# Memory key and value projections between the steps of the cross-attention, two probability buffers

## What is computed

```python
mk_p = jnp.einsum('bmd,ldk->lbmk', mem_prompt, w_mk)   # memory keys of the prompt, an output too
mv_p = jnp.einsum('bmd,ldk->lbmk', mem_prompt, w_mv)   # memory values of the prompt, an output too
...
def memory_attention(x, mem_k, mem_v, w_mq, w_mo):
    q = (x @ w_mq).reshape(bsz, T, MEM_HEADS, MEM_HD)            # 4 heads of 256
    s = jnp.einsum('bthd,bmhd->bhtm', q, mem_k) * (MEM_HD ** -0.5)
    p = jax.nn.softmax(s, axis=-1)
    o = jnp.einsum('bhtm,bmhd->bthd', p, mem_v)
    return o @ w_mo
...
x = layer_norm(DN_ALPHA * x + mix, ln_g[l, 0], ln_b[l, 0])
x = layer_norm(DN_ALPHA * x + memory_attention(x, mem_k[l], mem_v[l], w_mq[l], w_mo[l]), ln_g[l, 1], ln_b[l, 1])
x = layer_norm(DN_ALPHA * x + hier_moe(x, ...), ln_g[l, 2], ln_b[l, 2])
```

## Time and profile before

| | us |
|---|---|
| median of 3 runs | 1953.09 |
| lowest, highest | 1949.16, 1953.87 |
| profiled execution | 1948.43 |
| its span, first to last instruction | 1946.7 |
| PE, DVE, ACT busy in the span | 1541.0, 455.4, 297.1 |
| layer 0, end of the mixer's output projection to start of the attention's | 169.6 |
| layer 1, the same | 170.6 |

### The profile page before, as it was taken

One profiled execution on the slowest core, in us unless ns is written; L12 is line 12 of the kernel. 1 busy time (PEld: TensorE's weight loads), 2 busy tenths in 40 slices (PEclk: granted clock), 3 DMA queues, 4 the chain that ended last, 5 costly groups with the idle time before them and its releaser, 6 DMA issues.

```text
span 1946.7 us, 32778 instructions
## 1 busy us (share of the span) xinstructions
PE 1541.0 (79%) x14532; PEld 1001.6 (51%) x14532; DVE 455.4 (23%) x969; ACT 297.1 (15%) x530; POOL 107.1 (6%) x232
## 2 busy tenths in 40 slices
PE   8997899787967766777599878998779677567773
PEld 6766447545644534455275664466456355344550
DVE  0338400414111110111310664104141110101103
ACT  1233102302000000000122321113020000000001
POOL 3123100000000000000000321000000000000000
PEclk9987899886999889888699768998879988898886
DMA  9431333582999999999923323425828999999993
GB/s 343 146 130 52 113 140 110 207 364 76 384 418 417 421 422 420 418 417 420 351 87 130 101 82 114 151 108 187 362 99 357 418 416 423 422 419 419 417 421 120
DMA packets 118175, 536.42 MB, mean 276 GB/s; under 512 B 5614, under 2 KB 23054, under 8 KB 101648
## 3 DMA queue, kind: packets, MB, share of 16 engines
q1 hardware_dynamic: 113600, 519.98, 67.1%
q0 software_dynamic: 2704, 7.95, 1.3%
q10 hardware_dynamic: 1728, 6.29, 0.9%
HBM read 521.71 MB, written 12.49 MB: 274 GB/s over the span
## 4 chain that ended last, share of the span: by engine, by line
PE 48%; DMA 31%; DVE 8%; SPq 7%; ACT 3%; issue 2%; ACTq 0%; DVEq 0%; POOL 0%
PE ps L587 11%; DMA W<-in_w_gate 9%; DMA scr<-in_w_up 7%; SPq L393 7%; PE ps L633 6%; DMA W<-in_w_down 6%; PE ps L622 6%; PE ps L875 5%; DMA W<-in_w_up 4%; DMA scr<-in_w_down 4%; PE ps L859 3%; PE ps L602 2%; PE ps L715 2%; DVE scr L1274 2%; PE ps L884 2%
## 5 line engine op out<-in xcount | busy, mean ns | idle before, releaser
L875 PE MATMUL ps<-W,scr 128*32 128x128 f32 x6144 | 216.9, 303 | 76.0 <-issue 49.4
L875 PEld LDWEIGHTS ps<-W,scr 128*32 128x32 f32 x6144 | 192.0, 123 | 109.7 <-issue 69.1
L587 PE MATMUL ps<-XT,W 128*128 128x288 f32 x896 | 223.1, 412 | 3.3 <-ACT XT L995 2.8
L587 PEld LDWEIGHTS ps<-XT,W 128*128 128x128 f32 x896 | 172.0, 193 | 53.0 <-ACT XT L995 4.1
L884 PE MATMUL ps<-W,scr 128*32 128x512 f32 x768 | 118.0, 749 | 91.4 <-DMA W<-in_w_down 85.3
L859 PE MATMUL ps<-scr 128*128 128x128 f32 (+1 forms) x864 | 166.2, 326 | 0.9 <-DVE scr L1436 0.9
L1447 DVE TENSOR_TENSOR X<-X,ps 32x256 f32<-32x256 f32 x72 | 29.8, 414 | 526.9 <-PE ps L847 526.1
L859 PEld LDWEIGHTS ps<-scr 128*128 128x128 f32 (+1 forms) x864 | 126.9, 202 | 40.0 <-issue 11.0
L884 PEld LDWEIGHTS ps<-W,scr 128*32 128x32 f32 x768 | 23.7, 124 | 174.8 <-DMA W<-in_w_down 124.5
L622 PE MATMUL ps<-W,scr 128*128 128x512 f32 x256 | 110.3, 593 | 1.6 <-ACT scr L1023 1.6
L1157 ACT ACT_TABLE_LOAD x16 | 20.5, 1283 | 593.7 <-PE ps L875 593.7
(11 more groups left out here) (294 smaller groups left out, 1563.0 us busy)
## 6 DMA issues: line engine op xcount, KB each, us to landing
W<-in_w_gate SPq DMA_DIRECT2D x48, 2048.0 KB, 27.7
W<-in_w_up SPq DMA_DIRECT2D x48, 2048.0 KB, 31.0
W<-in_w_down SPq DMA_DIRECT2D x48, 2048.0 KB, 30.7
scr<-in_w_gate SPq DMA_DIRECT2D x16, 2048.0 KB, 24.0
scr<-in_w_up SPq DMA_DIRECT2D x16, 2048.0 KB, 29.1
scr<-in_w_down SPq DMA_DIRECT2D x16, 2048.0 KB, 37.1
scr<-in_cache_mem_k SPq DMA_DIRECT2D x16, 1024.0 KB, 6.9
scr<-in_cache_mem_v SPq DMA_DIRECT2D x16, 1024.0 KB, 5.9
```

What stands on the lines that cost most here:

```text
L587: last = mm(bank[:, 0:NT], w[:, k, c * P:(c + 1) * P], XT[:, k, :], start=(k == 0), stop=(k == KC - 1))
L875: last = mm(ps[j * CAP:(j + 1) * CAP, bank, e * P:(e + 1) * P], XG[:, k, e * CAP:(e + 1) * CAP], w[:, k, j * P:(j + 1) * P], start=(k == 0 ...
```

## The change

The order of the units becomes mq, mk, mv, mo, and the memory stage is planned after the queries. PE no longer runs the memory part as a whole: the four transposing jobs come after the queries, one key job after every second cached key, the prompt's keys are turned last, one value job follows the prompt scores, and three more lie between the first values. The transposed memory tokens go to `XT` (free once the queries are made), the new keys to `GB` (free once the norm is done), so the norm's next parameters are loaded later. The first three cache loads are issued at the end of the mixer, for which the mixer's output `o` moves out of their way. Each prompt tile has its probabilities in its own buffer, with its own small columns; ACT makes both tiles' exponentials before it copies anything of them out, and DVE does both maxima before the scalings.

```diff
-            for name in ("mk", "mv", "mq", "mo"):
+            for name in ("mq", "mk", "mv", "mo"):
...
+        PR = [KT0.rearrange("p k m -> p (k m)")[:, 0:MH * MEM].rearrange("p (h m) -> p h m", h=MH), PR1]
+        MEMT = XT[:, :, 0:MEM]
+        MK = GB
...
+            plan_xt(1 + 3 * l)
+            plan(("mq", l), *[("feat", f"mq{j}", c) for j in range(2) for c in range(4)])
             plan(("mem", l), *[("mt", i, h) for i in range(MT_) for h in range(2)])
             plan(("mem", l), *[("memtok", f"{w}{j}", i) for w in ("mk", "mv") for j in range(2) for i in range(MT_)])
-            plan_xt(1 + 3 * l)
-            plan(("mq", l), *[("feat", f"mq{j}", c) for j in range(2) for c in range(4)])
...
+                        sp.wait_ge(S("state_out"), count_at("state_out", l, 32 * HEADS))
+                        sp.wait_ge(S("rms"), count_at("rms", l, HEADS))
+                        for i in range(3):
+                            sp.dma_start(KV[i], caches[i]).then_inc(S(f"kv_in{i}"), 16)
...
+                for i in range(3, 2 * DB):
+                    if i < DB + 3:
+                        sp.wait_ge(S("kt_full"), count_at("kt_full", l, 4 * (i - 2)))
                     else:
-                        sp.wait_ge(S("pv_done"), count_at("pv_done", l, i - 3 - DB + 1))
+                        sp.wait_ge(S("pv_done"), count_at("pv_done", l, i - 2 - DB))
...
-                pool.wait_ge(S("pipe_free"), number(("mem", l)))
-                pool.dma_start(O["mem_k"][l, 0].rearrange("(i p) h d -> p i (h d)", p=P), KV[2]).then_inc(S("memk_out"), 16)
+                pool.wait_ge(S("pipe_free"), mem_done(l, MEM_JOBS // 2 - 1))
+                pool.dma_start(O["mem_k"][l, 0].rearrange("(i p) h d -> p i (h d)", p=P), MK[:]).then_inc(S("memk_out"), 16)
+                pool.wait_ge(S("pipe_free"), mem_done(l, MEM_JOBS - 1))
                 pool.dma_start(O["mem_v"][l, 0].rearrange("(i p) h d -> p i (h d)", p=P), VP).then_inc(S("memv_out"), 16)
...
-                pe.wait_ge(S("ln_done"), 3 * (3 * l) + TT)
-                turn_keys(0, KV[2])
                 run_jobs(("xt", 1 + 3 * l))
                 run_jobs(("mq", l))
+                run_jobs(("mem", l), jobs[("mem", l)][0:2 * MT_])
...
                 for b in range(DB):
                     pe.wait_ge(S(f"kv_in{b % 3}"), 16 * (kv_loads(l, b)))
-                    turn_keys(b + 1, KV[b % 3])
+                    turn_keys(b, KV[b % 3])
+                    if b % 2:
+                        run_jobs(("mem", l), mem_job(l, b // 2))
                     if b:
                         sample_scores(b - 1)
+
+                pe.wait_ge(S("pipe_free"), mem_done(l, MEM_JOBS // 2 - 1))
+                turn_keys(DB, MK)
                 sample_scores(DB - 1)
...
                 prompt_scores(0)
                 prompt_scores(1)
+                run_jobs(("mem", l), mem_job(l, MEM_JOBS // 2))
...
+                run_jobs(("mem", l), mem_job(l, MEM_JOBS // 2 + 1))
+                for b in range(2):
+                    sample_values(b)
+                run_jobs(("mem", l), mem_job(l, MEM_JOBS // 2 + 2))
+                sample_values(2)
+                run_jobs(("mem", l), mem_job(l, MEM_JOBS // 2 + 3))
                 prompt_values(0)
-                for b in range(3):
+                for b in range(3, 5):
                     sample_values(b)
                 prompt_values(1)
-                for b in range(3, DB):
+                for b in range(5, DB):
                     sample_values(b)
...
-                run_jobs(("mem", l))
                 attention(l)
...
+                prompt_exp(0)
+                empty_jobs(mem, mem_job(l, MEM_JOBS // 2))
                 act.wait_ge(S("spt_ps"), count_at("spt_ps", l, 1))
                 st.tell(fn(SST.rearrange("p i c -> p (i c)"), ps[:, 4, 0:MEM], ACT.Copy), S("spt_sb"))
+                prompt_exp(1)
+                act.wait_ge(S("memk_out"), count_at("memk_out", l, 16))
+                load_gb(2 + 3 * l)
+                for n in range(1, MEM_JOBS // 2):
+                    empty_jobs(mem, mem_job(l, MEM_JOBS // 2 + n))
+                for t in range(PT_):
+                    prompt_out(t)
...
-                norm(1 + 3 * l, range(PT_))
-                empty_jobs(("mem", l), part(("mem", l), upto="mk0"))
-                norm(1 + 3 * l, range(PT_, TT))
-                empty_jobs(("mem", l), part(("mem", l), after="mk0"))
+                norm(1 + 3 * l)
```

More of the change, by code:

```diff
@@ L193, in build @@
         at = r.at
-        PR = r.take(MH, MEM)
+        PR1 = r.take(MH, MEM)
         PRT = r.take(MT_, MH * P)
@@ L292, in part, with mem_job, mem_done @@
             return [j for j in jobs[stage] if lo <= j[0] < hi]
+        def mem_job(l, n):
+            return [jobs[("mem", l)][2 * MT_ + n]]
+        def mem_done(l, n):
+            return mem_job(l, n)[0][0] + 1
+        MEM_JOBS = 4 * MT_
         GATES, QUERIES = ("f", "gk"), ("q", "gk")
@@ L353, in _ @@
                 p_out = O[("hgrn_p", "gla_p")[l]][0, 0]
+                caches = [I[name][l, b].rearrange("(i p) h d -> p i (h d)", p=P) for name in ("cache_mem_k", "cache_mem_v") for b in range(DB)]
                 for n in range(start, end):
@@ L619, in run_jobs @@
                         w = wslot(l, name)
[L620 removed]
                         for k in range(KC):
[L622 removed]
+                            last = mm(bank, MEMT[:, k, c * P:(c + 1) * P], w[:, k, :], start=(k == 0), stop=(k == KC - 1))
                     last.then_inc(S("pipe_full"), 1)
@@ L1099, in keys @@
                         st.tell(fn(dst[:, 2 * j:2 * j + 2, :].rearrange("p c m -> p (c m)"), ps[:, j, :], ACT.Copy), S("kt_a"))
-                keys(0, KTP)
+                mem = ("mem", l)
                 empty_jobs(("xt", 1 + 3 * l))
-                load_gb(2 + 3 * l)
                 empty_jobs(("mq", l))
+                empty_jobs(mem, jobs[mem][0:2 * MT_])
                 for b in range(DB):
@@ L1107, in attention, with prompt_exp @@
                         act.wait_ge(S("ssc"), count_at("ssc", l, b - 1))
-                    keys(b + 1, KT[b % 2])
+                    keys(b, KT[b % 2])
+                    if b % 2:
+                        empty_jobs(mem, mem_job(l, b // 2))
+                keys(DB, KTP)
                 act.wait_ge(S("smax"), count_at("smax", l, 1))
                 st.tell(fn(SS, SS, ACT.Exp, bias=small[:, 0, 0:1], accum_out=small[:, 1, 0:1]), S("sexp"))
-                act.wait_ge(S("spt_ps"), count_at("spt_ps", l, 1))
-                st.tell(fn(SST.rearrange("p i c -> p (i c)"), ps[:, 4, 0:MEM], ACT.Copy), S("spt_sb"))
-                for t in range(PT_):
+                def prompt_exp(t):
                     act.wait_ge(S("pmax"), count_at("pmax", l, t + 1))
                     for h in range(MH):
-                        ins = fn(PR[:, h, :], ps[:, 2 * t + h // 2, (h % 2) * MEM:(h % 2 + 1) * MEM], ACT.Exp,
-                                 bias=small[:, 2, h:h + 1], accum_out=small[:, 3, h:h + 1])
+                        ins = fn(PR[t][:, h, :], ps[:, 2 * t + h // 2, (h % 2) * MEM:(h % 2 + 1) * MEM], ACT.Exp,
+                                 bias=small[:, 2 + 4 * t, h:h + 1], accum_out=small[:, 3 + 4 * t, h:h + 1])
                         if h < MH - 1:
@@ L1362, in attention, with prompt_max, prompt_scale @@
                 tell(ts(small[:, 0, 0:1], small[:, 0, 1:2], -1.0, None, ALU.mult), S("smax"))
+                def prompt_max(t):
+                    dve.wait_ge(S("psc"), count_at("psc", l, t + 1))
+                    step(red(small[:, 4 + 4 * t, 0:MH], ps[:, 2 * t:2 * t + 2, :].rearrange("p a (b m) -> p (a b) m", m=MEM), AX.X, ALU.max))
+                    tell(ts(small[:, 2 + 4 * t, 0:MH], small[:, 4 + 4 * t, 0:MH], -1.0, None, ALU.mult), S("pmax"))
+                def prompt_scale(t):
+                    dve.wait_ge(S("pexp"), count_at("pexp", l, t + 1))
+                    step(dve.reciprocal(small[:, 5 + 4 * t, 0:MH], small[:, 3 + 4 * t, 0:MH]))
+                    tell(tt(PR[t], PR[t], bc(small[:, 5 + 4 * t, 0:MH].unsqueeze(2), P, MH, MEM), ALU.mult), S("pr_ready"))
                 dve.wait_ge(S("sexp"), count_at("sexp", l, 1))
@@ L1366, in attention @@
                 for t in range(PT_):
-                    dve.wait_ge(S("psc"), count_at("psc", l, t + 1))
-                    step(red(small[:, 4, 0:MH], ps[:, 2 * t:2 * t + 2, :].rearrange("p a (b m) -> p (a b) m", m=MEM), AX.X, ALU.max))
-                    tell(ts(small[:, 2, 0:MH], small[:, 4, 0:MH], -1.0, None, ALU.mult), S("pmax"))
-                    dve.wait_ge(S("pexp"), count_at("pexp", l, t + 1))
-                    step(dve.reciprocal(small[:, 5, 0:MH], small[:, 3, 0:MH]))
-                    tell(tt(PR, PR, bc(small[:, 5, 0:MH].unsqueeze(2), P, MH, MEM), ALU.mult), S("pr_ready"))
+                    prompt_max(t)
+                for t in range(PT_):
+                    prompt_scale(t)
```

33 lines of the change are left out of this document (12 added, 21 removed).

## The result

The changed kernel takes 1917.6 us (median of 4 runs, 1916.4 to 1919.4) against 1951.1 beside it (1945.8 to 1953.9): a ratio of 0.983 with a 95% interval of 0.981 to 0.986. The forecast was 1924 in a range of 1915 to 1940.

The account below looks back on a forecast made before the run. Expert parts run at the pace of DMA loads, so moving their start moves the end. Shorter attention stretches (11.4 + 12.4) and warm projections (5.6) sum to 29.4 us off the median 1953.1: 1924, range 1915 to 1940.

Parts of the forecast that it names:

- Step 1: After the mixer's output projection: TensorE waits uncovered for the last tile's norm, 8.55 us.
- Step 2: Query projections: the 128 matmuls start at a cold clock and take 33.67 us, against 31.32 warm.
- Rival C: Query projections: the cold clock lasts through them, 29 us per layer more, 1982 us; chance 0.02.
- Steps 3 and 4: After the queries: memory transposes 2.34 us, then cached keys, four key jobs and prompt keys 53.99 us, without cache waits.
- Step 5: Prompt scores to attention's projection: 58.64 us against 48.78 before, taking in 27.6 us of value jobs for 9.9 us.
- Step 6: The attention's output projection starts warm instead of cold: 2.8 us saved per layer, 5.6 in all.
- Rival A: Value part: TensorE's clock falls before the attention's projection, so step 6's gain falls away, 1929 us; chance 0.22.
- A with all values cold: All values run at 1.2 GHz too: 8 us a layer more than in step 5, 1945 us; chance 0.05 within A's.
- Rival B: Value part: the value jobs hide nothing and it grows by all of 27.6 us, 1965 us; chance 0.05.
- Rival D: Expert part: load-bound, its ring still filling at the start, it absorbs the gain; chance 0.06, shared with late loads.

Follow-up runs that it names:

- the filler: The changed kernel with five idle 512-column matmuls on TensorE in the wait for the norm, into an unread PSUM bank: 1909.7 us, ratio 0.979 to before.
- second profile: The changed kernel profiled a second time, with nothing changed: span 1917.2 us.
- the late load: The changed kernel with its first three cache loads issued behind the last output weights instead of at the mixer's end: 1937.6 us, ratio 0.993 to before.

## Why the prediction was right, by its steps

Steps 1 to 6 against the changed kernel's trace, layer 0 and 1:

- Step 1, norm uncovered: 8.55 forecast, 8.56 and 8.56 measured. The second norm of the kernel before was the same operation in the same surroundings.
- Step 2, cold queries: 33.67 forecast, 32.99 and 32.87. The cause is shown by the filler. Rival C, a clock that stays low through the queries, did not occur: the clock is 0.90 from 254 to 256 us and 1.00 behind.
- Steps 3 and 4, transposes and keys: 56.33 forecast, 55.51 and 55.52. Two errors partly cancel: the transposes with their hand-overs took 2.98 us instead of 2.34 (283.98 to 286.96), the keys 52.54 instead of 53.99. I kept the 24.22 us of before, which held 0.6 us of waits for cache loads; they are gone.
- Step 5, prompt scores to projection: 59.6 with hand-overs, 58.96 and 60.19. In layer 1 the late cache load came that the step had allowed 1 to 2 us for; the chain there:

```profile
1344.85 1.91 PE ps L803 x32
...
1346.77 9.20 DMA scr<-in_cache_mem_v
...
1356.01 1.11 PE ps L803 x16
```

The load took 9.2 us instead of 5.9. In the second profile such a load stands in the chain of both layers. Of the sum's 17.7 us saved against 27.6 + 48.8 the runs give 11 to the jobs and 6 to the second buffer. The total was right, the share was not spelled out.
- Step 6, a warm projection: 2.8 per layer forecast, 2.8 and 2.4 measured. Rival A would have left its first half at 16 to 17 us; it takes 14.00 in every kernel with the jobs in the values. From the prompt scores to the projection the clock is 1.00, and tile 1's eight transposes take 1.04 us there, against 1.98 at a clock of 0.51 with one buffer. In the key part (286.96 to 339.50) the clock is 1.00 too. The Trainium skill (page "TensorE: Matmul & The Clock Gate", section "Part 4: PE-mode transpose") says that the full clock does not engage for transposes in transpose mode. The traces do not agree, if the kernel's `pe.transpose` runs in that mode, which they do not show. The price of A with all values cold was added up too small: 4.8 us doubled for two tiles are 9.6 us a layer before any value, not 8.
- Rival B, nothing hidden, needed less than 6 us hidden of 27.6; it was some 11, without what the buffer gives. Rival D did not occur: the parts between the stretches last as long as before, to 0.4 us.

The sum of 29.4 stands against 30.3 in the trace and 33.5 in the timed medians; the difference lies mainly in the runs of before, as said above. That 29.4 and 30.3 are so close is in part luck: the stretches and projections gave 32.3 us, and 2.3 us were lost ahead of them in layer 0, where the change moves no work of TensorE. (The prediction's "16 jobs" are twelve, the four and eight that it lists; its sum uses the right ones.) What the forecast missed is not in its range but in its view: it took the uncovered norm as the price of the gain. By the table the steps up to the prompt scores shrink by 23.7 and 23.4 us while 27.6 us of value jobs leave them, so the uncovered norm and the cold clock behind it cost some 4 us net per layer, and that could be won back. The version with two key jobs under the norm is shorter by 4.1 and 4.4 us per layer, the one with four by 2.3 and 3.6.

## What to carry to other kernels

Work without a predecessor was worth splitting here: a piece for each wait, rather than all of it in the longest one (1908.7 against 1919.0 us side by side). Five useless products in the short wait did about as well by the times. Price a cover by what ends last when it is gone, and look for a place in the same kernel where the same step already stands uncovered; it gave 8.55 us where 8.56 were measured. A wait of a few us on TensorE can cost itself and then some 2 us in what follows at the low clock (1.7 in the queries behind the norm, 2.5 in tile 1 behind the shared buffer, 2.2 in the key transposes behind the late load), so small late steps can come out larger than the wait.

## What the runs showed of the hardware

TensorE's clock fell to its lower level behind pauses of at most 0.74 us, and not each time. With key jobs under the norm the queries took 33.0 us in one layer and 31.3 in the other, in both kernels. In each the last memory job ends 4.2 us ahead of the queries, and between the two stand only the transposes of X, with pauses of 0.25, 0.33 and 0.74 us for ACT's copies. The windows of the kernel with four, at the transposes of X (to 275.5) and the start of the queries in layer 0, then at the same place of layer 1:

```profile
268.00:272.00 4.00, 3.75 (x13) 1.68 (x11) 0.00 (x0) 0.69 (x2) 0.00 (x0) 1.00 0.00 0
272.00:276.00 4.00, 2.93 (x22) 2.31 (x23) 0.00 (x0) 2.52 (x6) 0.76 (x1) 0.99 0.64 253
276.00:280.00 4.00, 4.00 (x12) 2.85 (x11) 0.00 (x0) 0.00 (x0) 0.00 (x0) 0.58 0.05 13
1234.00:1238.00 4.00, 2.94 (x22) 2.31 (x23) 0.00 (x0) 2.53 (x6) 0.75 (x1) 1.00 0.63 251
1238.00:1242.00 4.00, 4.00 (x19) 3.11 (x18) 0.00 (x0) 0.32 (x1) 0.00 (x0) 1.00 0.05 15
```

In layer 0 the clock goes from 0.99 to a mean of 0.58, with TensorE busy 2.93 of 4 us ahead. In layer 1 it stays at 1.00 behind the same instructions with the same pauses, busy 2.94 of 4 us. So neither the transposes nor the pauses decide by themselves, and what does stays open.
